# Second layer's gate and up by seven block products, with weight sums made in the first layer

## The chip, the cores and the metric

The kernel runs on 1 core of one Trainium2 chip. The metric is the device time of one execution in microseconds (us); less is better. Numbers are fp32; a matmul input is split into a high and a low fp32r part, and a product is three matmuls: high by high, high by low, low by high.

## The reference

Two layers of a diffusion transformer on 512 latent and 256 context tokens of width 1024. Each layer: modulated layer norm, one projection into four head groups (global attention, windowed attention, Fourier mix, retention), output projection, gated residual with norm; then the feed-forward part that the change touches:

```
def swiglu(h, w_gu, w_dn):
    g, u = jnp.split(h @ w_gu, 2, axis=-1)
    return (jax.nn.silu(g) * u) @ w_dn
```

h has 1024 columns, w_gu has 2 x 2816 columns, w_dn is 2816 x 1024. In the second layer only the 512 latent tokens are needed from here on.

## The kernel before, in words

Work is written per engine, and semaphores tie the engines together. SP loads weights, POOL splits them into high and low, PE (TensorE) multiplies, ACT and DVE read the results out of PSUM.

**Units and slots.** `plan` (L55) lists all weight loads in order. A unit is one load into one of the two halves of `stage` (L168); it holds four slots of 128 x 512. A unit's half is free again once all of its slots are split (`unit_release_wait`, L325). `split` (L755) runs on POOL: L757 writes the high part into a place of the ring, L760 writes stage minus high as the low part. The ring (`ring_hi`, `ring_lo`, L170) has 8 places, so slot g may be written when PE has used slot g - 8 (`ring_used`). PE waits for a slot by `w_ready`. `product` (L843 to L845) is the three matmuls; all weight products of the kernel have these lines.

**Gate and up** (`gate_up`, L1436). The 2816 columns are 22 chunks of 128 gate and 128 up columns, done in two halves of 11 (`gu0`, `gu1`), each followed by its part of the down projection (`dn0`, `dn1`). A chunk is one unit, four slots, each with two blocks of 128 of the 1024 rows of w_gu, for gate and up. In the first layer a chunk multiplies 768 tokens in two parts of 384 columns (96 matmuls); in the second 512 tokens at once (48 matmuls). Chunks 0 and 1 of `gu0` are done in parts of 256 tokens (`part`, L1468) while the norm before them ends; chunk 0 then has its own buffers (`own_hi`, `own_lo`). In the second layer tiles 2 and 3 of the tokens come first, then 4 and 5.

**Read-out.** ACT makes silu of a chunk's gate (`gate_half`, L2032; L2043), DVE multiplies it by up into `hid` (`up_half`, L2672; L2679). Chunks use two sets of PSUM banks in turn, so chunk f waits for the product of chunk f - 2. ACT and DVE split `hid` for down (L2030, L2184; `hid_high`, `hid_lows`). Between chunks DVE also adds up modulation vectors for later (`ffn_terms`, L2497; lines L2494, L2495) from `mod_stage`, loaded by ACT's queue; PE sums their columns in some chunks of the first layer.

**Order around the change.** Each engine's stream is in the order written. On SP: unit loads, each after the release of the unit two before, with bias rows in between (L668). The norm before gate and up (`norm_steps`) writes the modulated tokens of two tiles in turn into `hbuf` (L226), ACT makes `act_hi` and DVE `act_lo` (L2184) of them. Norm weights of a layer lie in rows 2 and 3 of `bc` (L227); `load_norm` (L2019) brings the second norm's after the first norm's steps (L2152).

## Time and profile before

| | |
|---|---|
| three runs, median (lowest to highest) | 1631.61 us (1630.08 to 1632.77) |
| the profiled execution, span from first to last instruction | 1629.1 us |
| median of the runs less that span | 2.5 us |
| mean granted TensorE clock | 0.999 |
| busy: PE, DVE, ACT, POOL | 1592.0, 783.9, 427.1, 855.8 us |

The profile is one execution on the core. Busy is the sum of an engine's instructions; the chain of waits is followed back from the last instruction. PE instructions overlap, so the pace of PE is read from the distance of two starts, not from the length of one. L numbers are lines of the kernel before. The profile gives the span of its execution, not its time between host marks, so the two are compared by the difference in the table.

### The profile page before, as it was taken

The page shows a single profiled execution, that of the slowest core. Times are in us where ns is not written, and L with a number is a line of the kernel's source. Part 1 is how long each engine was busy: PE and PEld are TensorE (multiplying, and loading weights), DVE is VectorE, ACT ScalarE, POOL GpSimd, SP SyncE. Part 2 cuts the span into 40 slices and gives each one's busy share as a digit, 9 for nine tenths or more (in the row PEclk, how much of TensorE's full clock was granted, in tenths as well). Part 3 has the DMA queues.
Part 4 walks back from the last instruction along what each step waited for, and adds up shares of the span by engine and source line. Part 5 has one row for each costly group of instructions (what it writes and reads, how often), then busy time and mean ns, then how long its engine had stood idle before and what let it go on. Part 6 is the DMA issues. An engine that isn't in the chain of part 4 may idle for free.

```text
span 1629.1 us, 23301 instructions
## 1 busy us (share of the span) xinstructions
PE 1592.0 (98%) x9335; PEld 1358.5 (83%) x9335; DVE 783.9 (48%) x1201; ACT 427.1 (26%) x920; POOL 855.8 (53%) x850
## 2 busy tenths in 40 slices
PE   7999999999999999999999999999999999999997
PEld 5788666778999988899999888886778888888886
DVE  4352265549663414443555396715659322520038
ACT  5512365425400011100002065216534200200011
POOL 4643044633464444544445455613485777777772
PEclk9999999999999999999999999999999999999999
DMA  9312143121453312244561121210032642233321
GB/s 343 118 52 78 41 149 118 57 78 52 119 165 92 117 40 78 67 146 124 177 210 60 66 78 53 78 52 9 15 85 74 195 142 91 90 95 101 104 91 52
DMA packets 161369, 160.89 MB, mean 99 GB/s; under 512 B 6520, under 2 KB 120296, under 8 KB 161264
## 3 DMA queue, kind: packets, MB, share of 16 engines
q1 hardware_dynamic: 140928, 121.40, 24.5%
q10 hardware_dynamic: 20336, 38.03, 7.2%
q8 instruction: 74, 1.21, 0.3%
q14 instruction: 31, 0.25, 0.0%
HBM read 157.31 MB, written 2.10 MB: 98 GB/s over the span
## 4 chain that ended last, share of the span: by engine, by line
PE 86%; DVE 7%; ACT 4%; issue 2%; DMA 1%; SPq 0%; DVEq 0%; POOL 0%; ACTq 0%
PE ps L843 24%; PE ps L845 24%; PE ps L844 24%; PE ps L1123 3%; PE ps L1147 2%; PE ps L1171 2%; ACT probs L1845 1%; DVE resid L2271 1%; DVE act_lo L2184 1%; DVE st L2212 1%; DVE ps L2193 1%; ACT hbuf L1647 1%; PE ps L966 1%; ACT probs_more L1845 1%; PE ps L927 1%
## 5 line engine op out<-in xcount | busy, mean ns | idle before, releaser
L757 POOL TENSOR_SCALAR ring_hi<-stage 128x512 fp32r<-128x512 f32 x352 | 245.3, 697 | 519.5 <-PE ps L845 450.0
L760 POOL TENSOR_TENSOR ring_lo<-stage,ring_hi 128x512 fp32r<-128x512 f32 x352 | 480.8, 1366 | 29.4
L843 PE MATMUL ps<-act_hi,ring_hi 128*128 128x384 f32 (+2 forms) x1088 | 379.1, 348 | 0.5 <-POOL ring_lo L760 0.5
L845 PE MATMUL ps<-act_hi,ring_lo 128*128 128x384 f32 (+2 forms) x1088 | 377.8, 347 | 0.0
L844 PE MATMUL ps<-act_lo,ring_hi 128*128 128x384 f32 (+2 forms) x1088 | 377.8, 347 | 0.0
L843 PE MATMUL ps<-ring_hi,act_hi 128*128 128x512 f32 (+1 forms) x711 | 280.6, 395 | 0.4 <-DVE act_lo L2184 0.4
L845 PE MATMUL ps<-ring_hi,act_lo 128*128 128x512 f32 (+1 forms) x711 | 273.5, 385 | 0.0
L844 PE MATMUL ps<-ring_lo,act_hi 128*128 128x512 f32 (+1 forms) x711 | 273.1, 384 | 0.0
L843 PEld LDWEIGHTS ps<-act_hi,ring_hi 128*128 128x128 f32 x1088 | 204.6, 188 | 13.9 <-POOL ring_lo L760 0.7
L845 PEld LDWEIGHTS ps<-act_hi,ring_lo 128*128 128x128 f32 x1088 | 204.5, 188 | 13.2
L844 PEld LDWEIGHTS ps<-act_lo,ring_hi 128*128 128x128 f32 x1088 | 204.6, 188 | 13.0
L2679 DVE TENSOR_TENSOR hid<-silu_g,ps 128x768 f32<-128x768 f32 (+1 forms) x44 | 36.1, 821 | 301.9 <-ACT silu_g L2043 301.6
L2043 ACT ACTIVATE silu_g<-ps 128x768 f32<-128x768 f32 (+1 forms) x44 | 31.1, 706 | 555.6 <-PE ps L845 525.6
L843 PEld LDWEIGHTS ps<-ring_hi,act_hi 128*128 128x128 f32 x711 | 133.7, 188 | 31.1 <-issue 4.0
L845 PEld LDWEIGHTS ps<-ring_hi,act_lo 128*128 128x128 f32 x711 | 133.5, 188 | 27.3
L844 PEld LDWEIGHTS ps<-ring_lo,act_hi 128*128 128x128 f32 x711 | 133.8, 188 | 26.3 <-issue 1.4
L770 POOL TENSOR_SCALAR probs<-probs,rden 128x768 f32<-128x768 f32 (+3 forms) x50 | 38.6, 779 | 128.9 <-DVE rden L2482 128.9
L2474 DVE TENSOR_REDUCE negmax<-ps 128x1 f32<-128x768 f32 (+4 forms) x80 | 58.0, 766 | 65.2 <-PE ps L1085 36.9
L2495 DVE SCALAR_TENSOR_TENSOR mod_acc_ffn<-mod_stage,c_silu,mod_acc_ffn 128x512 f32<-128x512 f32 x84 | 78.7, 963 | 18.8 <-DMA mod_stage<-in_w_mod_dram 17.0
L843 PE MATMUL ps<-ring_hi,hs_hi 128*128 128x512 f32 x220 | 86.6, 393 | 0.1
L845 PE MATMUL ps<-ring_hi,hs_lo 128*128 128x512 f32 x220 | 85.7, 389 | 0.0
L844 PE MATMUL ps<-ring_lo,hs_hi 128*128 128x512 f32 x220 | 85.6, 389 | 0.0
(278 smaller groups left out, 2046.1 us busy)
## 6 DMA issues: line engine op xcount, KB each, us to landing
stage<-in_w_gate_up_dram SPq DMA_DIRECT2D x88, 512.0 KB, 5.1
mod_stage<-in_w_mod_dram ACTq DMA_DIRECT2D x56, 512.0 KB, 4.2
stage<-in_w_in_dram SPq DMA_DIRECT2D x18, 1024.0 KB, 5.0
stage<-in_w_down_dram SPq DMA_DIRECT2D x16, 1024.0 KB, 5.0
stage<-in_w_mod_dram SPq DMA_DIRECT2D x12, 1024.0 KB, 5.2
start_mod<-in_w_mod_dram SPq DMA_DIRECT2D x16, 512.0 KB, 9.7
stage<-in_w_down_dram SPq DMA_DIRECT2D x8, 768.0 KB, 4.4
stage<-in_w_out_dram SPq DMA_DIRECT2D x16, 256.0 KB, 4.5
```

The lines of the kernel that those rows point to most:

```text
L757: nc.gpsimd.tensor_scalar(hi_, stage[:, par, j * 512:(j + 1) * 512], 1.0, 0.0, ALU.mult, ALU.add).then_inc(w_hi, 1)
L760: nc.gpsimd.tensor_tensor(lo_, stage[:, par, j * 512:(j + 1) * 512], hi_.bitcast(F32), ALU.subtract).then_inc(w_ready, 1)
L770: nc.gpsimd.tensor_scalar(probs_slot(2 * i + a)[:, 0:n], probs_slot(2 * i + a)[:, 0:n], rden[:, m:m + 1], 0.0, ALU.mult, ALU.add).then_inc ...
L843: nc.tensor.matmul(o, a_hi, b_hi, start=first, stop=False)
L844: nc.tensor.matmul(o, a_hi, b_lo, start=False, stop=False)
L845: return nc.tensor.matmul(o, a_lo, b_hi, start=False, stop=last)
L1123: last[a] = nc.tensor.matmul(flat[a][:, c0:c0 + m * P], qk[rows[a], b, t * P:(t + 1) * P], qk[rows[a], 2, k0 * P:(k0 + m) * P], start=True ...
L1147: mm = nc.tensor.transpose(ps[:, 4 + c, (j % 4) * P:(j % 4 + 1) * P], probs_slot(2 * i + a)[:, k * P:(k + 1) * P], ident[:, :])
L1171: mm = nc.tensor.matmul(ps[rows[a], 7, 0:P], v_attn[g][:, k, rows[a]], probs_T[1 - i % 2][:, (a * n + j) * P:(a * n + j + 1) * P], start=( ...
L2474: v.tensor_reduce(negmax[:, m:m + 1], flat[:, 0:n], AX, ALU.max, negate=True).then_inc(sem("neg_ready"), 1)
L2495: return v.scalar_tensor_tensor(acc, w, c_k, acc, ALU.mult, ALU.add)
L2679: done(v.tensor_tensor(hid[:, j, lo_col:TOK].rearrange("p (r n) -> p r n", **pat), silu_g[:, e, lo_col:TOK].rearrange("p (r n) -> p r n", ...
```

## The change

It replaces 19 of the second layer's 22 chunks of gate and up (chunks 3 to 10 of the first half and all 11 of the second), called fast chunks. A chunk's weights are a 2 x 2 block matrix (gate and up by two halves of the 1024 rows) and the tokens another (two halves of the rows by two halves of 256 tokens). Their product is formed from seven block products (Winograd's form) in place of eight, each of 4 blocks of 128 rows by 256 tokens, hence 4 x 3 matmuls of 256 columns.

- Four of the seven left factors are sums of weight blocks. POOL makes them (`weight_sums`) ahead of unit splits in the first layer's halves, from weights that SP loads for that into `pre_sum`, rows 2 and 3 of `bc`; SP stores them to DRAM (`send_sums`). The second norm's rows of the first layer are loaded only after the last store.
- A fast chunk has two units, of 4 and 3 slots (`send_fast`). ACT makes all seven high parts, DVE the low parts of slots 3 and 4, POOL the other five.
- The token sums are made by DVE (`t_sums`, `t_lows`) and ACT (`t_highs`) from `hbuf` and two more tile buffers, so `hbuf` isn't reused in that norm.
- PE's steps 4, 5 and 6 add onto PSUM banks that hold earlier products. ACT copies the first (`fast_copy`) and DVE forms the sums (`fast_half`).

```diff
+FIRST_FAST = {(DEPTH - 1, 0): 3, (DEPTH - 1, 1): 0}
+STEPS = 7
+FAST_FIRST = 4
+BY_DVE = (3, 4)
...
+def sum_units():
+    places = [UNIT0[(0, "gu0")] + f for f in range(2, HALF)] + [UNIT0[(0, "gu1")] + f for f in range(HALF)]
+    return places[:len(fast_chunks()) + 1]
...
+        def fast_left(u, i):
+            u, j = (u, {0: 0, 2: 1, 1: 2, 3: 3}[i]) if i < FAST_FIRST else (u + 1, {6: 0, 4: 1, 5: 2}[i])
+            return stage[:, u % 2, j * 512:(j + 1) * 512]
+        def fast_right(i):
+            first, second = slice(CTX, CTX + 256), slice(CTX + 256, TOK)
+            return {0: (act_hi[:, 0:4, first], act_lo[:, 0:4, first]),
+                    1: (act_hi[:, 0:4, 0:256], act_lo[:, 0:4, 0:256]),
+                    2: (act_hi[:, 4:8, 0:256], act_lo[:, 4:8, 0:256]),
+                    3: (t1_sets[:, 0, :, :], t1_sets[:, 1, :, :]),
+                    4: (act_hi[:, 4:8, first], act_lo[:, 4:8, first]),
+                    5: (t4_sets[:, 0:4, 0:256], t4_sets[:, 4:8, 0:256]),
+                    6: (act_hi[:, 4:8, second], act_lo[:, 4:8, second])}[i]
...
+            def send_sums(n):
+                if n:
+                    sp.wait_ge(sem("sums_made"), 4 * n)
+                    sp.dma_start(sums_dram[n - 1, :, :], pre_sum[:, :, :].rearrange("p b c -> p (b c)")).then_inc(sem("sums_stored"), 16)
+                if n == len(fast_chunks()):
+                    return
+                l, fh, f = fast_chunks()[n]
+                sp.wait_ge(sem("sums_stored"), 16 * n)
+                if n == 0:
+                    need(sp, "sum2", (0, 1), NT)
+                blocks = pre_sum[:, :, :].rearrange("p b (k c) -> p b k c", k=4)
+                gate, up = (gu_src(l, g, fh * HALF + f) for g in range(2))
+                sp.dma_start(blocks[:, 1, :, :], gate[:, 0:4, :]).then_inc(sem("sums_in"), 16)
+                sp.dma_start(blocks[:, 0, :, :], gate[:, 4:8, :]).then_inc(sem("sums_in"), 16)
+                sp.dma_start(pre_sum[:, 2:4, :].rearrange("p b (k c) -> p (b k) c", k=4), up).then_inc(sem("sums_in"), 16)
...
+                    def send_fast(u, f, n):
+                        first, second = (stage[:, v % 2, :].rearrange("p (b k c) -> p b k c", b=4, k=4) for v in (u, u + 1))
+                        unit_release_wait(sp, u - 2)
+                        sp.dma_start(first[:, 0, :, :], gu_src(l, 0, f)[:, 0:4, :]).then_inc(unit_in[u % 2], 16)
+                        sp.wait_ge(sem("sums_stored"), 16 * (n + 1))
+                        sp.dma_start(stage[:, u % 2, 512:2048], sums_dram[n, :, 512:2048]).then_inc(unit_in[u % 2], 16)
+                        unit_release_wait(sp, u - 1)
+                        sp.dma_start(second[:, 1, :, :], gu_src(l, 0, f)[:, 4:8, :]).then_inc(unit_in[(u + 1) % 2], 16)
+                        sp.dma_start(second[:, 2, :, :], gu_src(l, 1, f)[:, 4:8, :]).then_inc(unit_in[(u + 1) % 2], 16)
+                        sp.dma_start(stage[:, (u + 1) % 2, 0:512], sums_dram[n, :, 0:512]).then_inc(unit_in[(u + 1) % 2], 16)
...
+            def weight_sums(n):
+                pool.wait_ge(sem("sums_in"), 48 * (n + 1))
+                for m, (o, a, b, op) in enumerate(((3, 2, 3, ALU.add), (2, 1, 2, ALU.subtract), (1, 3, 1, ALU.subtract),
+                                                   (0, 0, 1, ALU.subtract))):
+                    if m:
+                        pool.wait_ge(sem("sums_made"), 4 * n + m)
+                    nc.gpsimd.tensor_tensor(pre_sum[:, o, :], pre_sum[:, a, :], pre_sum[:, b, :], op).then_inc(sem("sums_made"), 1)
+            def fast_low(l, u, g, i):
+                pool.wait_ge(ring_used, g - 7)
+                pool.wait_ge(sem("fast_hi"), slots_of((ACT_HIGH, DVE_LOW), g))
+                nc.gpsimd.tensor_tensor(ring_lo[:, g % RING, :], fast_left(u, i), ring_hi[:, g % RING, :].bitcast(F32),
+                                        ALU.subtract).then_inc(w_ready, 1)
...
+                    first = fast_part((l, seg), i)
+                    if first is not None:
+                        for j in range(first, first + n):
+                            if j not in BY_DVE:
+                                fast_low(l, u0 - (first > 0), g0 + j - first, j)
+                        g0 += n
+                        u0 += 1
+                        continue
...
+                    if u0 in sum_units()[:-1]:
+                        weight_sums(sum_units().index(u0))
...
+                def fast_chunk(g, f):
+                    c = fast_number(l, fh, f)
+                    if f >= 2:
+                        need(pe, "hid_ready", l, f0 + f - 1)
+                    elif f == 1:
+                        need(pe, "dn_read", l, 2 * len(tiles_of(l)))
+                    for i, (gu, r) in enumerate(((0, 0), (1, 0), (1, 1), (0, 1), (0, 0), (1, 0), (0, 1))):
+                        slot_wait(pe, g + i)
+                        if c == 0 and i in T_DONE:
+                            need(pe, "t_done", l, T_DONE[i])
+                        if i == 4:
+                            need(pe, "fast_copy", l, c + 1)
+                        elif i > 4:
+                            need(pe, "fast_read", l, 3 * c + i - 3)
+                        b_hi, b_lo = fast_right(i)
+                        for k in range(4):
+                            w = slice(k * P, (k + 1) * P)
+                            mm = joined(fast_bank(l, fh, f, gu, r), ring_hi[:, (g + i) % RING, w], ring_lo[:, (g + i) % RING, w],
+                                        b_hi[:, k, :], b_lo[:, k, :], i < 4 and k == 0, k == 3)
+                        mm.then_inc(ring_used, 1)
...
+            def fast_highs(l, fh, f):
+                g, u = gu_slot(l, fh, f), gu_unit(l, fh, f)
+                for i in range(STEPS):
+                    if i in (0, FAST_FIRST):
+                        unit_wait(act, u + i // FAST_FIRST)
+                    act.wait_ge(ring_used, g + i - 7)
+                    a.activation(ring_hi[:, (g + i) % RING, :], fast_left(u, i), ACT.Copy).then_inc(sem("fast_hi"), 1)
+                    if i == 0 and f and is_fast(l, fh, f - 1):
+                        fast_copy(l, fh, f - 1)
+            def fast_copy(l, fh, f):
+                c = fast_number(l, fh, f)
+                act.wait_ge(ring_used, gu_slot(l, fh, f) + 1)
+                need(act, "fast_read", l, 3 * c)
+                a.activation(one[:, :], fast_bank(l, fh, f, 0, 0), ACT.Copy).then_inc(sem("fast_copy"), 1)
+            def t_highs(l, ns):
+                for n in ns:
+                    i, j = T_ORDER[n]
+                    need(act, "t_ready", l, n + 1)
+                    src, dst = t_source(i, j), t_part(fast_right(i)[0], j)
+                    a.activation(dst, src, ACT.Copy).then_inc(sem("t_hi"), 1)
...
+                if (l, fh) == (DEPTH - 1, 0):
+                    t_highs(l, range(4))
                 for f in range(HALF):
+                    if f < HALF - 1 and is_fast(l, fh, f + 1):
+                        fast_highs(l, fh, f + 1)
                     if f == HALF - 1:
...
+                        if is_fast(l, fh, f):
+                            send_fast(u, f0 + f, fast_number(l, fh, f))
+                            continue
+                        unit_release_wait(sp, u - 2)
+                        send_gu(u, f0 + f)
                         if f in (1, 2) and seg == "gu0":
...
+                if fh == 0 and is_fast(l, 1, 0):
+                    fast_highs(l, 1, 0)
...
+                if l < DEPTH - 1:
+                    act.wait_ge(sem("sums_stored"), 16 * len(fast_chunks()))
+                    load_norm(l, ln2_w, ln2_b)
...
+            def t_sums():
+                k0, k1 = slice(0, 512), slice(512, D)
+                for j in range(2):
+                    done(v.tensor_tensor(h_more[j][:, k1], h_more[j][:, k1], h_more[j][:, k0], ALU.subtract), "t_ready")
+                for j in range(2):
+                    done(v.tensor_tensor(h_more[j][:, k0], h_more[j][:, k0], hbuf[:, j, k0], ALU.subtract), "t_ready")
+                for j in range(2):
+                    ins = v.tensor_tensor(hbuf[:, j, k0], hbuf[:, j, k0], h_more[j][:, k1], ALU.add)
+                done(ins, "t_ready")
+            def t_lows(l):
+                k0, k1 = slice(0, 512), slice(512, D)
+                done(v.tensor_tensor(hbuf[:, :, k1], hbuf[:, :, k1], hbuf[:, :, k0], ALU.subtract), "t_ready")
+                for n, (i, j) in enumerate(T_ORDER):
+                    need(dve, "t_hi", l, n + 1)
+                    if i == 5:
+                        dve.wait_ge(ring_used, gu_slot(l, 0, 1))
+                    hi_, lo_ = (t_part(x, j) for x in fast_right(i))
+                    done(low(lo_, t_source(i, j), hi_), "t_done")
+            def fast_lows(l, fh, f, which):
+                u, g, c = gu_unit(l, fh, f), gu_slot(l, fh, f), fast_number(l, fh, f)
+                for i in which:
+                    dve.wait_ge(ring_used, g + i - 7)
+                    need(dve, "fast_hi", l, STEPS * c + i + 1)
+                    done(low(ring_lo[:, (g + i) % RING, :], fast_left(u, i), ring_hi[:, (g + i) % RING, :]), "fast_lo")
+            def fast_half(l, fh, f, between):
+                g, c = gu_slot(l, fh, f), fast_number(l, fh, f)
+                _, g2, u1, u2 = (fast_bank(l, fh, f, gu, r) for gu in range(2) for r in range(2))
+                more = f < HALF - 1
+                def after(i):
+                    dve.wait_ge(ring_used, g + i + 1)
+                after(2)
+                need(dve, "fast_copy", l, c + 1)
+                done(v.tensor_tensor(both[:, :], one[:, :], u2, ALU.add), "fast_read")
+                done(v.tensor_tensor(one[:, :], both[:, :], u1, ALU.add), "fast_read")
+                after(3)
+                done(v.tensor_tensor(u2, one[:, :], g2, ALU.add), "fast_read")
+                if more:
+                    fast_lows(l, fh, f + 1, BY_DVE)
+                between()
+                after(5)
+                link(v.tensor_tensor(u1, both[:, :], u1, ALU.add))
+                after(6)
+                done(v.tensor_tensor(g2, both[:, :], g2, ALU.add), "fast_gate")
...
+                if (l, fh) == (DEPTH - 1, 0):
+                    t_sums()
                 for f in range(HALF):
+                    if is_fast(l, fh, f):
+                        fast_half(l, fh, f, first_slices if f == HALF - 1 else lambda: ffn_terms((l, fh), f))
+                        need(dve, "silu_ready", l, fh * HALF + f + 1)
+                        chunk(f)
+                        continue
                     if f == HALF - 1:
```

Not shown: the bookkeeping of slots by kind (`slot_wait`: a fast slot whose low DVE makes is waited for by `fast_lo`, any other by `w_ready`), `joined` (as `product`, without the group check), and the order in which `t_highs` go on ACT: the first four before chunk 0's silu, two after it. In the last chunk of a half DVE does the first `hid_lows` (1 in the first half, 4 in the second) between step 3's and step 5's sums.

## Rows read from the trace of the kernel before

**Rows 1.** The page: busy us by engine, and the chain that ended last.
```profile
PE 1592.0 (98%) x9335; PEld 1358.5 (83%) x9335; DVE 783.9 (48%) x1201; ACT 427.1 (26%) x920; POOL 855.8 (53%) x850
...
PE 86%; DVE 7%; ACT 4%; issue 2%; DMA 1%; SPq 0%; DVEq 0%; POOL 0%; ACTq 0%
```

**Rows 2.** Windows (us): length, busy by engine, PE clock, DMA share, GB/s.
```profile
690.00:880.00 190.00, 190.00 (x1119) 189.86 (x1118) 92.44 (x109) 11.98 (x15) 89.66 (x88) 1.00 0.48 148
1291.00:1379.00 88.00, 88.00 (x390) 72.84 (x389) 19.78 (x23) 6.33 (x12) 66.67 (x68) 1.00 0.40 120
1440.00:1561.00 121.00, 121.00 (x536) 100.19 (x535) 15.82 (x21) 9.06 (x16) 86.25 (x90) 1.00 0.33 94
```

**Rows 3.** Timeline of ACT, second layer's second half: start, length, what.
```profile
1473.18 0.60 ACT L2043 ACTIVATE silu_g<-ps 128x512 f32<-128x512 f32 x1 [10.28 <-PE ps L845]
...
1549.34 0.60 ACT L2043 ACTIVATE silu_g<-ps 128x512 f32<-128x512 f32 x1 [10.28 <-PE ps L845]
```

**Rows 4.** Timeline of PE, second and 49th of a row of 256 column matmuls.
```profile
1268.96 0.28 PE L844 MATMUL ps<-act_lo,own_hi 128*128 128x256 f32 x1
...
1274.59 0.28 PE L843 MATMUL ps<-act_hi,ring_hi 128*128 128x256 f32 x1
```

**Rows 5.** Groups by line, 1291 to 1561: count, busy us, mean ns, idle before.
```profile
L760 POOL TENSOR_TENSOR ring_lo<-stage,ring_hi 128x512 fp32r<-128x512 f32 x101 | 134.8, 1334 | 8.5
L757 POOL TENSOR_SCALAR ring_hi<-stage 128x512 fp32r<-128x512 f32 x100 | 66.8, 668 | 63.0 <-PE ps L845 62.1
L2184 DVE TENSOR_TENSOR hs_lo<-hid,hs_hi 128x512 fp32r<-128x512 f32 x19 | 22.1, 1163 | 23.8 <-ACT hs_hi L2030 23.6
L2030 ACT ACTIVATE hs_hi<-hid 128x512 fp32r<-128x512 f32 x19 | 11.8, 630 | 36.6 <-PE ps L845 36.5
```

**Rows 6.** DMA issues, 1440 to 1561: count, size, median landing; L728's extremes, whole span.
```profile
stage<-in_w_gate_up_dram SPq DMA_DIRECT2D x16, 512.0 KB, 5.0
stage<-in_w_down_dram SPq DMA_DIRECT2D x2, 1024.0 KB, 4.9
DMA to landing us min/median/max: 3.8/5.1/7.0
```

**Rows 7.** Timeline of DVE: a first-layer low, then the second layer's first chunks.
```profile
410.42 2.20 DVE L2184 TENSOR_TENSOR act_lo<-hbuf,act_hi 128x1024 fp32r<-128x1024 f32 x1
...
1267.99 1.42 DVE L2184 TENSOR_TENSOR act_lo<-hbuf,act_hi 128x512 fp32r<-128x512 f32 x2 [0.77 <-ACT act_hi L1660]
1275.49 0.69 DVE L2679 TENSOR_TENSOR hid<-silu_g,ps 128x512 f32<-128x512 f32 x1 [6.08 <-ACT silu_g L2043]
1276.21 1.50 DVE L2494 TENSOR_SCALAR bc<-mod_stage,c_silu 128x512 f32<-128x512 f32 x1
1277.75 0.75 DVE L2495 SCALAR_TENSOR_TENSOR bc<-mod_stage,c_silu,bc 128x512 f32<-128x512 f32 x1
...
1281.97 2.07 DVE L2495 SCALAR_TENSOR_TENSOR bc<-mod_stage,c_silu,bc 128x512 f32<-128x512 f32 x2
```

**Rows 8.** Timeline where the first half goes over to down.
```profile
1378.30 0.39 PE L843 MATMUL ps<-ring_hi,hs_hi 128*128 128x512 f32 x1
...
1379.92 1.91 DVE L2184 TENSOR_TENSOR hs_lo<-hid,hs_hi 128x512 fp32r<-128x512 f32 x2
...
1381.25 0.47 PE L843 MATMUL ps<-ring_hi,hs_hi 128*128 128x512 f32 x1
```

**Rows 9.** First layer: POOL's lows (group, 436 to 880; one), chunk products, a store.
```profile
L760 POOL TENSOR_TENSOR ring_lo<-stage,ring_hi 128x512 fp32r<-128x512 f32 x105 | 145.0, 1381 | 8.8
...
400.49 2.13 POOL L760 TENSOR_TENSOR ring_lo<-stage,ring_hi 128x512 fp32r<-128x512 f32 x1
...
706.66 0.95 DVE L2679 TENSOR_TENSOR hid<-silu_g,ps 128x768 f32<-128x768 f32 x1 [12.22 <-ACT silu_g L2043]
...
880.23 0.96 DVE L2679 TENSOR_TENSOR hid<-silu_g,ps 128x768 f32<-128x768 f32 x1 [5.37 <-ACT silu_g L2043]
...
out_dram<-resid SPq DMA_DIRECT2D x3, 512.0 KB, 2.7
```

More of the change, by code:

```diff
@@ L47, with is_fast, fast_number, fast_chunks @@
 START_TILES = [2, 3, 0, 4, 1, 5]
-def segment(key):
-    return [-4] * 2 + [4] * 7 if key == (1, "win") else SEGMENTS[key[1]]
+FIRST_FAST = {(DEPTH - 1, 0): 3, (DEPTH - 1, 1): 0}
+STEPS = 7
+FAST_FIRST = 4
+BY_DVE = (3, 4)
+def is_fast(l, fh, f):
+    return f >= FIRST_FAST.get((l, fh), HALF)
+def fast_number(l, fh, f):
+    return sum(is_fast(l, h, j) for h in range(2) for j in range(HALF) if (h, j) < (fh, f))
+def fast_chunks():
+    return [(l, h, f) for l in range(DEPTH) for h in range(2) for f in range(HALF) if is_fast(l, h, f)]
+def gu_units(l, fh, f):
+    return sum(2 if is_fast(l, fh, j) else 1 for j in range(f))
+def segment(key):
+    if key == (1, "win"):
+        return [-4] * 2 + [4] * 7
+    if key[1][:2] == "gu":
+        fast = [is_fast(key[0], int(key[1][2]), f) for f in range(HALF)]
+        return sum(([FAST_FIRST, STEPS - FAST_FIRST] if one else [4] for one in fast), [])
+    return SEGMENTS[key[1]]
+def fast_part(key, i):
+    if key[1][:2] != "gu":
+        return None
+    place = i - FIRST_FAST.get((key[0], int(key[1][2])), HALF)
+    return None if place < 0 else FAST_FIRST * (place % 2)
 def plan():
-    order = []
+    order, kinds = [], []
     for l in range(DEPTH):
@@ L845, in product, with joined @@
                 return nc.tensor.matmul(o, a_lo, b_hi, start=False, stop=last)
+            def joined(o, a_hi, a_lo, b_hi, b_lo, first, last):
+                nc.tensor.matmul(o, a_hi, b_hi, start=first, stop=False, skip_group_check=True)
+                nc.tensor.matmul(o, a_hi, b_lo, start=False, stop=False, skip_group_check=True)
+                return nc.tensor.matmul(o, a_lo, b_hi, start=False, stop=last, skip_group_check=True)
             def keep_clock(bank, n):
@@ L2067, in gate_half @@
                             hid_high(l, 2 * fh, j)
-                    chunk(f, g0 + 4 * f + 4, fh * HALF + f - 1 if f >= 2 else None)
+                    chunk(f, gu_slot(l, fh, f) + 4, fh * HALF + f - 1 if f >= 2 else None)
+                    if (l, fh, f) == (DEPTH - 1, 0, 0):
+                        t_highs(l, range(4, 6))
                     load_mods(f)
@@ L2711, in down_low @@
                         link(half_stats(t, 0, 0))
+                if fh == 0 and is_fast(l, 1, 0):
+                    fast_lows(l, 1, 0, BY_DVE)
                 if fh == 0:
```

125 lines of the change are left out of this document (91 added, 34 removed).

## The prediction

> **What bounds the kernel now.** I read the page's busy times and its chain first, then a table by stage, then the timelines of the stretches that change. TensorE is busy 98% of the span and carries 86% of the chain [rows 1]: time is gained only where its stream gets shorter, lost where another engine makes it wait. The changed stretches are the second layer's two gate and up halves, and in both TensorE is busy for the whole window at granted clock 1.00 (the 2.4 GHz level), POOL for 71 to 76% [rows 2]. A chunk there takes 10.88 us: eight silus from 1473.18 to 1549.34 are seven equal periods [rows 3], and a chunk is 48 matmuls of 512 columns, so 226.7 ns each. In the first layer's halves TensorE is full too; POOL works 89.66 of 190 us there [rows 2], so it has room for the weight sums.
>
> **The products.** A fast chunk issues 7 x 4 x 3 = 84 matmuls of 256 columns for 48 of 512. The trace has such matmuls, each with its own weights, at the start of this layer's gate and up: from 1268.96 to 1274.59 are 47 intervals, 120 ns each [rows 4]. Their weight loads are in that pace. So 84 x 0.120 = 10.08 us against 10.88: 0.80 us less, although columns fall by an eighth (1.36 us), since each matmul costs 13.3 ns beyond its columns and there are 36 more. Chunks 3 to 10 of the first half and all 11 of the second are fast: 19 x 0.80 = **15.2 us gained**.
>
> The Trainium skill ("TensorE: Matmul & The Clock Gate", Back-to-back issue gap) gives an isolated gap of columns/2.4 + 2.5 ns. By that 84 are 9.2 us and 48 are 10.4 us, an estimate of 1.2 us a chunk and 22.5 us in all. The rows show 120 and 226.7 ns for this stream, so the trace does not agree and decides.
>
> **Who prepares the operands.** Before, POOL did both parts of 4 slots a chunk, 4 x (0.67 + 1.33) = 8.0 us [rows 5]. Now ACT copies 7 highs, 7 x 0.63 = 4.4, plus a quarter-size PSUM copy and silu 0.60 [rows 3]: under 5.5 us of 10.08. POOL subtracts 5 lows: 6.7 us. DVE has 2 lows (2 x 1.16), five combinations of 256 columns (0.4 each at most; half the 0.69 of the 512 wide read of PSUM in rows 7), the product 0.69, in the first half some terms: 5.0 to 7 us. None is the bound by its sum. The combinations of one chunk end before their PSUM halves are wanted (step 5 wants step 2's sums, 2.9 us later).
>
> **The loop that can be the bound.** Slots 0 to 3 of a fast chunk are one stage buffer. Its next load may start only when these four are split, and PE's step 4 needs a copy that ACT makes behind the *next* chunk's first high, that is behind that landing. So landing leads to landing: ACT high 0.63, three POOL lows 3 x 1.33 with 0.1 of semaphores = 4.8 us (DVE's low of slot 3 ends about then), then the load. It is 1 MB in two DMAs; two 512 KB ones of a unit land in 5.0 us at the median, 3.8 to 7.0, a single 1 MB one in 4.9 [rows 6]. I take 5.2. Sum 10.0, against 10.08 of PE: level. Bounds: 3.8 gives 8.6 (nothing lost), 7.0 gives 11.8 (1.7 a chunk). The second half starts with the buffer loaded during down, and its second load goes out when slot 3's low is done, 7.7 us into chunk 0, and lands 2.9 us into chunk 1. PE stops only if a landing comes more than 4.7 us in (the copy is wanted at 5.76, a high and the copy take 1.0), so small drifts cost nothing. I take 1.0 us in all.
>
> Port contention goes against this. A DVE subtraction of 512 columns with both inputs in SBUF takes 0.71 us beside an idle POOL (two in 1.42, rows at 1267.99), and 1.16 on average [rows 5, 7]; one of 1024 columns took 2.20 beside a busy POOL [rows 7]. The Trainium skill ("SBUF — State Buffer", Who interferes with whom) has it as a lock: a DVE instruction with two SBUF inputs and a GpSimd one that reads SBUF block each other for a whole instruction. The trace agrees; it adds nothing to the sum. One of the loop's three POOL lows at the 2.13 that a blocked one took [rows 9] makes the loop 10.8.
>
> **Entry of the first fast chunk.** DVE must make the token sums before it: six 512 wide, from the last low's end at 1269.4 (4.3 to 7.0 us); after chunk 0's product, one 1024 wide, four lows 512 wide and two 1024 wide (7.0 to 11.3 us). Behind them wait chunk 0's terms, chunk 1's product, its terms (2.3 + 0.7 + 2.1 [rows 7]) and the low of slot 3. That low ends between 1289.0 and 1294.7; the next load (5.1) and its high and copy (1.0) follow, to 1295.1 or 1300.8. PE starts the chunk at 1291.2 and wants the copy at 1297.0. Stall 0 to 3.8 us; I take **2.0**.
>
> **Ends of the halves.** Silu now waits for a last DVE sum (0.4 and a hand-over), so the last product comes 0.5 us later. In the first half slot 1's low comes right after it, and PE waited for it already: 2.95 us between its first matmul and that one, for 12 matmuls worth 2.72 [rows 8]. In the second, four 1.16 us lows stand ahead of the last sums on DVE and push them past the chunk's end by about 1.5. 0.5 each, **1.0**; bounds 0 and 3.
>
> **First layer.** Each of 19 sets adds to POOL four 512 wide instructions, 4 x 1.38 = 5.5 us [rows 9], to SP one 1 MB store and three loads of 1 MB together, with SP waiting for the sums and for the store. Behind SP's waits stand the next gate and up unit and bias rows; behind POOL's wait for the loads the next unit's splits, and PE behind them. Set to set: store 4 (512 KB land in 2.7 [rows 9]), loads 6, sums 5.8 = 15.8 us; POOL's work a chunk is 8.3 + 5.5 = 13.8. PE's chunks come every 17.36 (ten from 706.66 to 880.23 [rows 9]), and the ring lets POOL lead by 7 slots of 4.34 us, so a late set is covered. DMA share was 0.48 [rows 2] and would be about 0.87 if each byte cost the same, so latencies will grow. Bounds of a set: 2.7 + 3.8 + 5.2 = 11.7; 5.4 + 7.8 (the last of three loads issued 0.8 later) + 4 x 2.13 = 21.7. I charge **0.4**. The second norm's rows load after the last store, over 60 us before their use: nothing.
>
> **Sum.** 15.2 - 1.0 - 2.0 - 1.0 - 0.4 = 10.8. The span was 1629.1, so 1618.3; the runs' median stands 2.5 above it, so **1620.8 us**.
>
> **Rivals.**
> *The buffer loop paces the chunks.* At 10.5 us a chunk the 19 save 7.2, less entry and ends 3.0: 1627.4. For it: the sum above is level with no margin, and the lock. Against: landings hold at 5.0 in this very half [rows 6], and a load of long rows should not be slower than one of short ones. Chance 0.25 (1624 to 1631).
> *All of it hides:* 15.2, 1616.4. For: POOL leaves DVE free more often now that ACT takes the highs. Chance 0.10.
> *The sums' round trip starves the first layer* (slower than before). SP's store, its wait, the loads and POOL's sums are one serial loop. At 21.7 us a set PE loses 4.3 a chunk once POOL's lead of 30 us is spent: 8 sets 35 - 30 = 5, 11 sets 48 - 30 = 18, so 23 us: 1644. It decides from about 21 us a set. For: DMA share 0.87. Against: store and load never run together in it. Chance 0.08.
> *The change doesn't do what it says:* the shorter matmuls lose their pace among step changes and operands from six places, say 128 ns: 10.75 a chunk, 2.5 saved, 1629 to 1635. Rows 4 speak against. Chance 0.05.
> *Each matmul costs its columns alone:* 19 x 48 x 512/2400 less 19 x 84 x 256/2400 is 24.3 us, 1611. The rows' 13.3 ns exclude it nearly: 0.02. (It is close to the isolated-gap rule of the Trainium skill, "TensorE: Matmul & The Clock Gate", Back-to-back issue gap.)
>
> **How the numbers follow.** Forecast (1617.5 to 1623.5) 0.50. The rest: 0.25, 0.10, 0.08, 0.05, 0.02. The range 1616 to 1629 takes in the hidden case and most of the loop's, and leaves out the first-layer case and the tails. 0.2% is 3.3 us, about what a measurement tells from no change. Faster (under 1628.3): 0.50 + 0.10 + 0.02 + 0.20 of the loop's + 0.01 of the slower matmuls' = 0.83. Same: 0.05 + 0.04 = 0.09. Slower 0.08.
>
> **What would show it.** Right: silu periods of 10.1 us in fast chunks, 256 column matmuls 120 ns apart within steps; one wait of PE of about 2 us on ACT's copy in the first half's chunk 3; first-layer periods unchanged at 17.36 on average; POOL busy some 104 us more there (19 x 5.5), less in the second layer. Wrong: periods of 10.4 or more with PE waiting at step 4 in each chunk (the loop); first-layer periods above 17.4 on average with PE waiting for POOL's lows (the sums); intervals over 0.12 us inside a step (the products).

## The result, and the profile after

Four runs of the changed kernel have a median of 1639.9 us (1633.5 to 1642.8), against 1631.0 (1630.1 to 1632.8) for the kernel before: ratio 1.0049 [1.0028, 1.0070]. It is slower by 9 us where 1620.8 was forecast. The profiled execution is the quickest of the four, with a span of 1631.3 us; the spans of the others are 1636.8 to 1640.6. So this trace shows only part of the loss, and a second profile of the same kernel (after_again, span 1643.2) stands beside it. Below, the quickest trace is the first of the two.

The page after, answering to [rows 1]:

```profile
PE 1583.2 (97%) x10019; PEld 1382.2 (85%) x10019; DVE 931.7 (57%) x1347; ACT 510.4 (31%) x1078; POOL 965.1 (59%) x869
...
PE 73%; DVE 11%; DMA 6%; ACT 5%; issue 3%; POOL 2%; SPq 0%; ACTq 0%; DVEq 0%; POOLq 0%
```

TensorE is less busy in time, as meant, but its share of the chain fell from 86% to 73%, and DMA, 1% before, has 6%. The windows of [rows 2], after:

```profile
690.00:880.00 190.00, 187.93 (x1099) 187.84 (x1098) 111.45 (x107) 11.29 (x14) 141.99 (x119) 0.99 0.72 231
1291.00:1379.00 88.00, 81.37 (x641) 79.47 (x640) 63.41 (x76) 38.31 (x74) 58.80 (x40) 0.98 0.59 195
1440.00:1561.00 121.00, 119.42 (x954) 116.91 (x952) 70.08 (x97) 54.82 (x103) 83.26 (x59) 1.00 0.52 170
```

PE was busy for the whole of each before. Now it stops in all three, in the first layer too, where the DMA share went from 0.48 to 0.72 and 148 GB/s became 231 (a packet counts where it starts, so a short window can show a share over 1). What it waited for, in the second profile (line, releaser, total us, times, longest):

```profile
PE ps L1035 <- ACT one L2262: 11.2, 8, 4.2
...
PE ps L1079 <- DVE mod_acc_ffn L2752: 4.3, 1, 4.3
...
PE ps L1035 <- POOL ring_lo L936: 1.6, 1, 1.6
```

L1035 is a fast chunk's first matmul line, L2262 the copy that step 4 wants, L1079 the column sums of modulation vectors. The profile of the quickest run has 6.4 us in 6 waits, 2.1 and 1.5 in these lines.

**The products** are as forecast. The pace inside a step, and the silus of the second half, answering to [rows 4] and [rows 3]:

```profile
1523.42 0.28 PE L1037 MATMUL ps<-act_hi,ring_lo 128*128 128x256 f32 x1
1523.54 0.28 PE L1035 MATMUL ps<-t_sets,ring_hi 128*128 128x256 f32 x1
1523.66 0.28 PE L1036 MATMUL ps<-t_sets,ring_hi 128*128 128x256 f32 x1
```

```profile
1458.49 0.60 ACT L2286 ACTIVATE silu_g<-ps 128x512 f32<-128x512 f32 x1 [1.34 <-DVE ps L2980]
...
1552.76 0.60 ACT L2286 ACTIVATE silu_g<-ps 128x512 f32<-128x512 f32 x1 [1.74 <-DVE ps L2980]
```

120 ns a matmul, across the change of step as well; but nine silu periods are 94.27 us, 10.47 each. The 19 fast chunks of this trace take 202.7 us where 19 x 10.08 is 191.5 and the old chunks took 206.7: of 15.2 us, 4.0 are left. In after_again they take 208.7 us, longer than the old ones: nothing is left.

**The first layer's second half** ran from 706.66 to 880.23 before [rows 9], 173.57 us. After:

```profile
705.81 0.95 DVE L2989 TENSOR_TENSOR hid<-silu_g,ps 128x768 f32<-128x768 f32 x1 [12.22 <-ACT silu_g L2286]
...
883.16 0.95 DVE L2989 TENSOR_TENSOR hid<-silu_g,ps 128x768 f32<-128x768 f32 x1 [5.37 <-ACT silu_g L2286]
```

177.35, and 181.63 in the second profile. The chain of waits of the quickest run shows the place:

```profile
820.27 7.03 DMA mod_stage<-in_w_mod_dram
...
827.40 1.10 DVE mod_acc_ffn L2752
...
828.52 0.99 DVE mod_acc_ffn L2752
...
829.56 1.05 PE ps L1079 x8
```

The load of the last terms took 7.03 us, these came late, and PE's column sums behind them. Before, the load in this place was issued at 822.68 and the terms started at 826.60, 3.9 us later. The rows of before, then the window 820 to 825 of before and of after:

```profile
822.68 2.37 ACTq L2057 DMA_DIRECT2D mod_stage<-in_w_mod_dram  x2
...
826.60 1.54 DVE L2495 SCALAR_TENSOR_TENSOR mod_acc_ffn<-mod_stage,c_silu,mod_acc_ffn 128x512 f32<-128x512 f32 x2 [1.96 <-DMA mod_stage<-in_w_mod_dram]
```

```profile
820.00:825.00 5.00, 5.00 (x31) 5.00 (x30) 4.41 (x4) 0.00 (x0) 2.73 (x3) 1.00 0.24 59
```

```profile
820.00:825.00 5.00, 5.00 (x31) 5.00 (x30) 1.86 (x2) 0.00 (x0) 2.93 (x3) 1.00 1.14 335
```

Before, the 16 matmuls of the column sums ran as one row (first fence below); in the second profile the last eight waited, and the granted clock followed (windows with the columns of [rows 2]):

```profile
827.38 1.86 PE L887 MATMUL ps<-ones,mod_acc_ffn 128*128 128x1 f32 x16
```

```profile
827.61 0.95 PE L1079 MATMUL ps<-ones,mod_acc_ffn 128*128 128x1 f32 x8
832.90 1.44 PE L1079 MATMUL ps<-ones,mod_acc_ffn 128*128 128x1 f32 x6 [4.33 <-DVE mod_acc_ffn L2752]
```

```profile
825.00:830.00 5.00, 3.56 (x25) 3.48 (x23) 2.49 (x2) 0.00 (x0) 4.77 (x5) 1.00 0.98 320
830.00:835.00 5.00, 2.10 (x9) 2.11 (x10) 2.85 (x4) 0.81 (x1) 3.87 (x3) 0.54 0.43 134
835.00:840.00 5.00, 5.00 (x17) 5.00 (x17) 3.14 (x5) 0.00 (x0) 0.00 (x0) 0.50 1.02 371
840.00:845.00 5.00, 5.00 (x29) 5.00 (x28) 1.34 (x2) 0.00 (x0) 1.92 (x2) 0.93 0.37 122
```

At 835 to 840 PE is busy throughout but runs 17 matmuls where 840 to 845 has 29: half speed, the 1.2 GHz level. One wait of 4.3 us costs 8.1 in all; in the quickest run 2.1 us cost 3.8. In the trace of before the last of those terms ended at 828.14 (826.60 and 1.54), and PE wanted it about 0.2 us later, half-way through its row of 16.

**The buffer loop,** ACT's and SP's timelines in the second half of the quickest run:

```profile
1524.20 0.63 ACT L2253 ACTIVATE ring_hi<-stage 128x512 fp32r<-128x512 f32 x1 [3.25 <-DMA stage<-weight_sums]
1524.74 0.36 ACT L2262 ACTIVATE one<-ps 128x256 f32<-128x256 f32 x1
...
1535.46 0.63 ACT L2253 ACTIVATE ring_hi<-stage 128x512 fp32r<-128x512 f32 x1 [4.10 <-DMA stage<-weight_sums]
1536.00 0.37 ACT L2262 ACTIVATE one<-ps 128x256 f32<-128x256 f32 x1
```

```profile
1529.27 0.37 SPq L876 DMA_DIRECT2D stage<-in_w_gate_up_dram  x1
1529.68 0.91 SPq L878 DMA_DIRECT2D stage<-weight_sums  x1
1532.23 0.37 SPq L880 DMA_DIRECT2D stage<-in_w_gate_up_dram  x1
```

From one landing to the next is 11.26 us: 5.1 until the buffer is free, then 6.2 for the load, with the second unit's load started 3.0 us behind it. This is one of the two longest of the half: its nine periods from landing to landing are 10.15 to 11.27, 10.63 on average, with 5.1 until the buffer is free nearly every time and loads of 5.1 to 5.3 us (six) or 5.6 to 6.2 us (four). Each time the copy for step 4 comes right after the first high of the next chunk, so after the landing.

**The entry of the first fast chunk,** ACT's timeline:

```profile
1290.22 0.60 ACT L2286 ACTIVATE silu_g<-ps 128x512 f32<-128x512 f32 x1 [7.35 <-DVE bc L2752]
1293.21 0.38 ACTq L2300 DMA_DIRECT2D mod_stage<-in_w_mod_dram  x1
1293.69 3.75 ACT L2253 ACTIVATE ring_hi<-stage 128x512 fp32r<-128x512 f32 x7 [2.87 <-DVE bc L2752]
...
1303.77 0.63 ACT L2253 ACTIVATE ring_hi<-stage 128x512 fp32r<-128x512 f32 x1 [5.85 <-DMA stage<-weight_sums]
1304.31 0.36 ACT L2262 ACTIVATE one<-ps 128x256 f32<-128x256 f32 x1
```

ACT stood 7.35 and 2.87 us in its own stream, waiting to issue modulation loads until DVE had used the ones before; DVE was at the token sums first, then at chunk 1's product and terms. ACT's highs, the next load and the copy all came late. That chunk took 14.79 us, 3.4 us of it at granted clock 0.50, and began 1.7 late.

### The profile page after: what moved, and what is told of

It reads as the page before. It is cut to its first block, busy times and chain, and to the rows that moved or that the text cites. A ratio compares the mean times of both kernels' runs of the same rounds, so it can differ in the third digit from the quotient of the medians.

```text
span 1631.3 us, 25476 instructions
## 1 busy us (share of the span) xinstructions
PE 1583.2 (97%) x10019; PEld 1382.2 (85%) x10019; DVE 931.7 (57%) x1347; ACT 510.4 (31%) x1078; POOL 965.1 (59%) x869
## 4 chain that ended last, share of the span: by engine, by line
PE 73%; DVE 11%; DMA 6%; ACT 5%; issue 3%; POOL 2%; SPq 0%; ACTq 0%; DVEq 0%; POOLq 0%
PE ps L1029 18%; PE ps L1031 18%; PE ps L1030 18%; DMA stage<-weight_sums 3%; PE ps L1315 3%; PE ps L1339 2%; DMA mod_stage<-in_w_mod_dram 2%; PE ps L1035 2%; PE ps L1037 2%; PE ps L1036 2%; POOL ring_lo L936 2%; DVE act_lo L2441 2%; PE ps L1363 2%; ACT probs L2059 1%; DVE st L2469 1%
## 5 line engine op out<-in xcount | busy, mean ns | idle before, releaser
L1029 PE MATMUL ps<-act_hi,ring_hi 128*128 128x384 f32 (+2 forms) x784 | 261.4, 333 | 0.5 <-POOL ring_lo L920 0.5
L1031 PE MATMUL ps<-act_hi,ring_lo 128*128 128x384 f32 (+2 forms) x784 | 260.3, 332 | 0.0
L1030 PE MATMUL ps<-act_lo,ring_hi 128*128 128x384 f32 (+2 forms) x784 | 260.2, 332 | 0.0
L930 POOL TENSOR_TENSOR pre_sum<-pre_sum 128x512 f32<-128x512 f32 x76 | 114.5, 1506 | 62.7 <-DMA pre_sum<-in_w_gate_up_dram 58.2
L1029 PEld LDWEIGHTS ps<-act_hi,ring_hi 128*128 128x128 f32 x784 | 148.1, 189 | 2.1 <-POOL ring_lo L920 0.7
L1031 PEld LDWEIGHTS ps<-act_hi,ring_lo 128*128 128x128 f32 x784 | 148.0, 189 | 1.3
L1030 PEld LDWEIGHTS ps<-act_lo,ring_hi 128*128 128x128 f32 x784 | 148.0, 189 | 1.2
L1035 PE MATMUL ps<-act_hi,ring_hi 128*128 128x256 f32 x380 | 108.8, 286 | 8.2 <-ACT one L2262 6.4
L1037 PE MATMUL ps<-act_hi,ring_lo 128*128 128x256 f32 x380 | 107.6, 283 | 0.0
L1036 PE MATMUL ps<-act_lo,ring_hi 128*128 128x256 f32 x380 | 107.6, 283 | 0.0
```

What stands on the lines that cost most here:

```text
L930: nc.gpsimd.tensor_tensor(pre_sum[:, o, :], pre_sum[:, a, :], pre_sum[:, b, :], op).then_inc(sem("sums_made"), 1)
L1029: nc.tensor.matmul(o, a_hi, b_hi, start=first, stop=False)
L1030: nc.tensor.matmul(o, a_hi, b_lo, start=False, stop=False)
L1031: return nc.tensor.matmul(o, a_lo, b_hi, start=False, stop=last)
L1035: nc.tensor.matmul(o, a_hi, b_hi, start=first, stop=False, skip_group_check=True)
L1036: nc.tensor.matmul(o, a_hi, b_lo, start=False, stop=False, skip_group_check=True)
```

## The experiments

Three groups of runs, each with the kernel before on the same chip (medians 1631.2, 1631.3 and 1631.0). All start from the changed kernel.

**after_again:** no edit, a second look.

> The changed kernel unaltered, for its spread over executions and a second trace. Theory A (in the first layer the traffic of the weight sums delays the loads of modulation weights, PE then waits for DVE's sums of them, and falls to the 1.2 GHz level for 3.4 us): executions between 1633 and 1643 us, and the lower the granted clock the longer; a trace of a longer execution has two to four such waits in the first layer's second half, where the first trace had one (2.1 us and 3.4 us at the lower level). Theory B (the spread comes from the fast chunks' loop of loads): the first layer is as in the first trace and fast chunks 3 to 10 of the first half are longer.

1641.9 us (1638.2 to 1645.4, 6 runs), ratio 1.0062 [1.0048, 1.0076]. This is the size of the loss; its waits are shown above. Neither theory has it alone: the first layer has one wait, not two to four, but of 4.3 us where the quickest trace had 2.1, and the half takes 4.3 us longer than in that trace; the fast chunks take 6.0 us longer.

**one_set:** only the first of 19 sets of sums is loaded, made and stored, and every fast chunk reads that one.

```diff
 def send_sums(n):
+    if n > 1: return
...
-    if n == len(fast_chunks()):
+    if n:
         return
...
-    sp.dma_start(stage[:, u % 2, 512:2048], sums_dram[n, :, 512:2048])
+    sp.dma_start(stage[:, u % 2, 512:2048], sums_dram[0, :, 512:2048])
 def weight_sums(n):
+    if n: return
```

> Only the first of the 19 sets of weight sums is loaded, made and stored; every fast chunk reads that one set (so most products are of wrong sums). Theory A: the first layer's second half goes back to the pace of the kernel before (silu to silu from chunk 0 to 10 in 173.6 us, changed kernel 177.3), the spread goes, and the time is 1628 to 1630 us. Theory B: the first layer gains the 3.7 us of the first trace at most, spread stays, median 1635 or more.

1634.9 (1630.8 to 1637.4, 11 runs), 1.0020 [1.0012, 1.0029]. The first layer's second half is back at 173.55 us without a wait at L1079. 6.9 us of after_again's time are in the making of the sums, loads and stores included. Theory A had the place, but its 1628 to 1630 left out the faults of the second layer, which stay.

**dma_only:** the loads and stores of the sets stay, POOL's sums go.

```diff
-    sp.wait_ge(sem("sums_made"), 4 * n)
+    sp.wait_ge(sem("sums_in"), 48 * n)
 def weight_sums(n):
+    return
```

> All 19 loads and stores of the weight sums stay, POOL's four instructions a set are left out (what is stored is not the sums). Theory A (traffic alone): as the changed kernel, median 1637 to 1641 us, waits of PE for modulation sums in the first layer stay. Rival C (POOL's sums and DVE's modulation terms block each other at the SBUF port, and DVE is late for that): the waits go, median 1628 to 1632 us.

1639.3 (1637.5 to 1644.7, 6 runs), 1.0056 [1.0043, 1.0069]. The wait at L1079 is there, 3.73 us, and the half takes 179.98. So the transfers alone bring the wait: it needs neither POOL's 5.5 us a set nor a lock of DVE by POOL. They may add a little, since the last two terms take 2.10 us in the changed kernel and 1.54 here; the time differs from after_again's by 2.5 us, within their spread, and no run makes the sums without the transfers.

**copy_first:** ACT copies PSUM for step 4 before it waits for the next load.

```diff
 for i in range(STEPS):
+    if i == 0 and f and is_fast(l, fh, f - 1):
+        fast_copy(l, fh, f - 1)
     if i in (0, FAST_FIRST):
         unit_wait(act, u + i // FAST_FIRST)
...
-    if i == 0 and f and is_fast(l, fh, f - 1):
-        fast_copy(l, fh, f - 1)
```

> ACT's copy of a fast chunk's first bank goes ahead of its wait for the next chunk's load. Theory D (the loop of loads reaches PE only through that copy at step 4): waits at step 4 go, fast chunks come every 10.08 us but for the first, 6.5 us less than the changed kernel and 2 to 4 us more at the first fast chunk: 8 to 10 us below the changed kernel's median. Rival E (the loop, at 10.3 us or more, moves the wait to step 0 of the next chunk, where its first slot is wanted): fast chunks at 10.3 us and more stay, gain under 3 us.

1638.7 (1635.0 to 1638.9, 5 runs), 1.0038 [1.0026, 1.0050]. Nine of the second half's 11 chunks take 10.08 us, the others 10.36 and 10.15: there the loop reached PE through the copy alone. In the first half 6.4 us of waits in 4 places remain, and the wait at L1079 is 4.3. There the copy stands behind other waits of ACT: for the first fast chunk behind the issue of a modulation load that waits 5.25 us for DVE's terms, later behind a silu that waits 4 to 5 us for DVE's last sums. So the run gains 3 us only, where 8 to 10 were expected.

**late_sum:** the column sums of one item are issued a chunk later.

```diff
 def ffn_sum_chunk(half, n):
-    return last + (3 if (half, n) == ((0, 0), 0) else 2)
+    return last + (3 if (half, n) in (((0, 0), 0), ((0, 1), 5)) else 2)
```

> PE's column sums of the last modulation item of the first layer's second half come one chunk later; the traffic of the weight sums stays. Theory A (the traffic hurts by that one wait and the lower level behind it): no wait there, silu to silu of that half 173.6 us, 5 to 8 us below the changed kernel: 1633 to 1636. Rival F (the traffic also costs elsewhere in that half, or the wait moves to a later place): pace stays over 175 us, gain under 3 us.

1634.3 (1630.5 to 1636.6, 12 runs), 1.0018 [1.0009, 1.0027], with all traffic in place. The clock and PE in the windows shown for after_again:

```profile
825.00:830.00 5.00, 5.00 (x34) 5.00 (x33) 3.19 (x4) 0.00 (x0) 4.83 (x5) 1.00 0.72 211
830.00:835.00 5.00, 5.00 (x31) 5.00 (x30) 3.48 (x5) 0.81 (x1) 3.39 (x3) 1.00 0.65 211
835.00:840.00 5.00, 5.00 (x31) 5.00 (x30) 2.38 (x4) 0.00 (x0) 1.91 (x2) 1.00 0.81 283
```

The half takes 173.55. One number in the order of work gives back 7.5 us of after_again's time (5.6 of the first four runs' 1639.9), as much as taking the sums away.

**copy_silu:** the copy goes just ahead of the silu of the chunk before, far from any load. Its two old places go, and that for the second half's chunk 0 stands ahead of the loop.

```diff
 for f in range(HALF):
...
+    if f < HALF - 1 and is_fast(l, fh, f + 1):
+        fast_copy(l, fh, f + 1)
     chunk(f, ...)
```

> ACT's copy for chunk f+1 goes ahead of the silu of chunk f. Theory G (in the first half, where ACT's copy stood behind a silu that DVE's terms had delayed, that order is all that was left of waits in chunks 4 to 10): these come every 10.1 us, 2 to 3 us less than with the copy ahead of the load alone; the first fast chunk keeps its 5 us. About 1636. Rival H (DVE itself is full in that half, about 10.7 us of work and waits a chunk): the waits move to the sums of PSUM halves at steps 5 and 6 and stay 0.5 to 1 us a chunk.

1637.6 (1635.2 to 1641.2, 6 runs), 1.0041 [1.0029, 1.0054]. The waits for the copy are gone, and others stand in their place, one step on:

```profile
PE ps L1035 <- DVE one L2971: 6.9, 4, 3.5
...
PE ps L1079 <- DVE mod_acc_ffn L2752: 5.4, 1, 5.4
```

DVE's sums that step 5 adds to are late, all four times in the first half, where DVE has the modulation terms as well. The waits moved one step on, as rival H says.

**all_three:** late_sum and copy_silu, and in the first half's three old chunks DVE does the terms before the product, so that ACT's loads are released sooner.

```diff
 # up_half, chunks that are not fast
+    if (l, fh) == (DEPTH - 1, 0):
+        ffn_terms((l, fh), f)
     need(dve, "silu_ready", l, fh * HALF + f + 1)
...
-    ffn_terms((l, fh), f)
+    if (l, fh) != (DEPTH - 1, 0):
+        ffn_terms((l, fh), f)
```

> Late column sums, the copy ahead of silu, and, in the second layer's first half, DVE's modulation terms of chunks 0 to 2 ahead of these chunks' products and of the token sums' second part, so that ACT is not held by its loads of modulation weights when it should split for the first fast chunk. Theory: the wait at the first fast chunk falls from 5 or 6 us to under 2, and the time to 1622 to 1627 us, below the kernel before. Rival (the token sums alone are too long for DVE): 3 us or more stay at the first fast chunk, 1627 to 1632.

1626.4 (1624.9 to 1628.3, 7 runs), 0.9973 [0.9963, 0.9984]: faster than the kernel before by 4.9 us in that group. The changed stretches, to set beside those above:

```profile
690.00:880.00 190.00, 190.00 (x1119) 189.78 (x1118) 113.45 (x109) 12.11 (x15) 141.44 (x121) 1.00 0.74 232
1291.00:1379.00 88.00, 83.33 (x675) 82.55 (x675) 65.33 (x79) 36.51 (x70) 59.91 (x43) 0.98 0.59 195
1440.00:1561.00 121.00, 121.00 (x969) 118.95 (x968) 78.16 (x103) 55.58 (x103) 84.23 (x61) 1.00 0.52 171
```

The first layer and the second half are full again, the latter with 11 chunks of 10.08. The first half still has 7.0 us over 8 x 10.08. The first fast chunk's wait is 1.0 us, as the theory has it, but the second's is 2.6.

**all_three_one_set:** one_set with all_three's copy and entry order.

> The copy and term order of all_three with only one set of weight sums made (every fast chunk reads it, so most products are of wrong sums). If the first layer's traffic costs nothing once the column sums come later, this is within 2 us of all_three; if it still costs, it is more than 3 us faster.

1628.4 (1624.1 to 1629.1, 11 runs), 0.9979 [0.9970, 0.9987]. Without 18 of the 19 sets it is no faster than all_three (2.0 us slower, for which no trace shows a cause): once the column sums have room, the sets cost the first layer nothing that shows.

**no_terms:** all_three with the first half's terms cut to 8 of 512 columns.

```diff
+w = slice(0, 8 if half == (DEPTH - 1, 0) else 512)
-ins = term(acc[:, o, :], mod_stage[:, u % 2, k, :], ...
+ins = term(acc[:, o, w], mod_stage[:, u % 2, k, w], ...
```

> all_three with the modulation terms of the second layer's first half cut to 8 of 512 columns (the second gate is wrong then); their loads stay. Theory I (what is left of waits in that half, 4.2 us and a fall of the clock in the trace of all_three, is DVE's load: its terms take 1.67 us each beside POOL): fast chunks 3 to 10 all at 10.1 us, 3 to 5 us faster than all_three, 1621 to 1623. Rival J (the waits come from the loads or from the copy): they stay, within 1 us of all_three.

1622.8 (1621.5 to 1624.0, 5 runs), 0.9951 [0.9938, 0.9963], 3.6 us less than all_three. PE's waits for DVE fall from 4.7 to 1.5 us; 2.5 us over 10.08 a chunk remain, so theory I's "all at 10.1" didn't come. The terms of all_three, then of no_terms, groups of the first half (count, busy us, mean ns), and the timelines of DVE and POOL in no_terms, with two terms beside an idle POOL first:

```profile
L2752 DVE SCALAR_TENSOR_TENSOR bc<-mod_stage,c_silu,bc 128x512 f32<-128x512 f32 x11 | 18.3, 1665 | 0.4
```

```profile
L2752 DVE SCALAR_TENSOR_TENSOR bc<-mod_stage,c_silu,bc 128x8 f32<-128x8 f32 x11 | 13.0, 1185 | 0.4
```

```profile
1286.48 0.49 DVE L2752 SCALAR_TENSOR_TENSOR bc<-mod_stage,c_silu,bc 128x8 f32<-128x8 f32 x2
...
1313.88 1.15 DVE L2751 TENSOR_SCALAR bc<-mod_stage,c_silu 128x8 f32<-128x8 f32 x1
1315.07 1.21 DVE L2752 SCALAR_TENSOR_TENSOR bc<-mod_stage,c_silu,bc 128x8 f32<-128x8 f32 x1
...
1313.71 2.55 POOL L936 TENSOR_TENSOR ring_lo<-stage,ring_hi 128x512 fp32r<-128x512 f32 x2 [0.57 <-ACT ring_hi L2253]
```

Eight columns still take 1.2 us beside POOL, where two took 0.49 together without it. The last one ends at 1316.28, as POOL's second low does (1316.26): most of such a term's time is waiting for POOL, not work. With terms of 8 columns DVE is still held for 13.0 us, so what the terms cost in all may be more than 3.6 us.

**low4_pool:** POOL instead of DVE makes slot 4's low in the first half.

```diff
-BY_DVE = (3, 4)
+BY_DVE = ((3,), (3, 4))
```

> all_three with the low part of slot 4 in the first half on POOL (6 lows) and one on DVE. Theory I: DVE is relieved by 1.4 us a chunk and the waits of chunks 4 to 8 go, 2 to 3 us faster than all_three, 1623 to 1625. Rival K (POOL, at 8.6 us and more a chunk, is then the later one, or the lock gives the time back): within 1 us of all_three or slower.

1626.2 (1624.0 to 1628.7, 6 runs), 0.9971 [0.9960, 0.9983]: all_three's time. Two waits of 4.5 us together stand where there were four of 4.7. The work taken from DVE gave no time back; by which way the gain was lost, POOL's longer list or the lock, the run doesn't tell.

**copy_silu_late:** all_three without the entry order.

> all_three without the moved modulation terms of chunks 0 to 2: what their place costs. Theory (ACT's loads wait for them and its splits for the first fast chunk stand behind): PE's wait for POOL's first low at chunk 3 (1.5 us) comes back and the one at chunk 4 is as long as in copy_silu (3.5 us): 3 to 5 us slower than all_three, 1630 to 1631. Rival: it is the number of DVE instructions that counts, not their place: within 1.5 us.

1628.8 (1627.0 to 1630.6, 11 runs), 0.9987 [0.9978, 0.9996]. The entry order is worth 2.4 us (3 to 5 were expected), and the copy's place, from late_sum to this kernel, 5.5.

**entry_copy_late:** all_three with copy_first's place of the copy.

> all_three with the copy ahead of the next chunk's load but behind silu. If the copy's place relative to silu matters (DVE's lateness reaches PE at step 4 by silu and copy), 1 to 3 us slower than all_three; if DVE's own sums at step 5 are the limit either way, within 1 us, the waits one step earlier.

1628.6 (1626.7 to 1631.6, 11 runs), 0.9986 [0.9977, 0.9995], 2.2 us over all_three. PE waits for the copy six times, 6.2 us, where all_three has 4.7 for DVE's sums. (The two traces are the slowest run of this kernel and the quickest of all_three, so they may overstate the difference.)

## Why the prediction was wrong

From after_again's 1641.9 the medians go down in steps: column sums later 1634.3, copy's place 1628.8, entry 1626.4, terms 1622.8. The forecast was 1620.8. The steps are each one comparison, all over two groups of runs (their kernels before differ by 0.3 us at most); by the spread of the runs the two small ones are good to about 2 us and the two large ones to about 4.

Three terms of the sum were too small, and none explains the miss alone: with the first layer whole again (late_sum) the time is still 1634.3. By the traces, quickest and after_again, in us beyond what was charged: first layer 3.4 and 7.7, loop 5.5 and 10.1, entry 4.4 and 5.7. The spans were 13.0 and 24.9 over the forecast's 1618.3.

- **Products (15.2 gained): right.** 120 ns in every unstalled step, chunks of 10.08 us, all 11 of them in all_three's second half.
- **First layer (0.4 charged): the step whose mechanism failed; it lost 3.8 and 8.1 us, and late_sum gives back 7.5.** The text asked whether POOL's lead covers a set, and it does: no profile has PE waiting there for POOL's lows. But it followed the new transfers to one queue only. "Latencies will grow" stands in it, and was not carried to the modulation loads of ACT's queue, whose chain (load, DVE terms, column sums on PE) had 0.2 us to spare in the trace of before. Their median landing in 700 to 880 went only from 4.2 to 4.6 us and the longest from 6.6 to 7.7, but the load that the last terms need took 7.03 where it had taken 3.9. The clock then about doubled the loss. dma_only shows that it needs no work of POOL; one_set and late_sum each bring back 173.55.
- **Loop (1.0 charged): the mechanism right, the size wrong, and the largest of the three.** Of the quickest trace's fast chunks after the first, the excess over 10.08 is 6.5 us, all at step 4; of after_again's it is 11.1. The text put the loop at 10.0, level with PE, and let small drifts cost nothing; from landing to landing it was 10.63 on average in the quickest trace's second half. Most loads took the 5.2 us forecast and four 5.6 to 6.2; the buffer was free after 5.1 where 4.8 was taken, with POOL's lows 1.44 where 1.33 was. Whether the second unit's load beside it lengthens the first, no run tests. All of it was within the bounds given. The place of the copy made each late landing a wait; moving it is worth 5.5 us. In the first half the copy also waited for DVE by way of silu (copy_first), which the text didn't have.
- **Entry (2.0 charged): the wait came, its price was 6.4 us** in the quickest trace (14.79 less 10.08, and 1.7 of late start). The text looked at DVE's queue and left out ACT's: ACT waits for DVE's terms before it issues a load, and behind that wait stood a silu and seven highs. The entry order gives back 2.4, and 1.7 us of the 6.4 are the clock (3.4 us at half speed); the rest wasn't taken apart. In after_again the same reckoning gives 7.7.
- **Ends (1.0 charged): about right.** PE waits 1.2 us for the lows at the first half's end, and some 0.5 at the second's.
- **POOL (104 us more):** 76 sums of 1.51 us are 114.5 in the quickest trace, a tenth over the forecast.

Of the rivals, the one that was slower than before (the sets' round trip) had the place, the first layer, and the sets as the cause, but not the path: PE never waited there for POOL's lows. The loop rival (10.5 a chunk, 1627.4) describes the second half well, 10.47 between silus. The range failed because the first layer was allowed to lose only through POOL, and because the loop and a loss in the first layer were rivals in it and never came together.

Open: why the spread between runs grew (9 us here, 3 before); it goes with the length of the waits and of the low clock after them, but no run sets these, and like waits had different ends (see the last section). Nor is the last 7.0 us of the first half divided between DVE's terms, its lows and the late start; a run without POOL beside DVE wasn't made.

## What to carry to other kernels

Before adding traffic to a full stretch, list every queue that loads in it and read the slack of each chain that ends at the bounding engine: here a chain with 0.2 us to spare broke, though the new work itself was covered. A loop that comes out level with the bounding engine has no margin: reckon its spread as a loss. An operation that reads early data should not stand in its engine's stream behind a wait for a load, or behind an issue that itself waits: the copy's place was worth 5.5 us and the entry's 2.4. When a change with a sound gain comes out slower, look for such places before undoing it: three edits of order turned +9 us into -4.9.

## What the runs showed of the hardware

**A stop of PE of about 2 us cost its own length or nearly twice that.** Waits of 2.1 and 4.3 us in the first layer went with 3.4 and 10.2 us at granted clock 0.50 (partly within the wait), for 3.8 and 8.1 us lost in all. All 14 waits of 2.64 us or more in the feed-forward stretches, over all traces, had such a low stretch with them or right behind. Of waits of 1.7 to 2.63 us some had one (1.81 in low4_pool, 1.92 in after_again) and some had none (2.13 in after_again, 1.67 and 2.08 in entry_copy_late). The closest pair is the second fast chunk's wait for DVE's sums, 2.64 us in all_three and 2.63 in all_three_one_set; the window behind each:

```profile
1313.00:1318.00 5.00, 5.00 (x32) 5.00 (x31) 4.70 (x4) 1.67 (x3) 5.00 (x4) 0.66 0.37 127
```

```profile
1315.00:1320.00 5.00, 5.00 (x44) 5.00 (x43) 4.89 (x4) 1.42 (x3) 5.00 (x4) 1.00 0.35 121
```

The matmuls started in 5 us are 32 in one and 44 in the other.

**DVE beside POOL waits whole instructions.** A term of 512 columns took 0.75 us alone [rows 7] and 1.67 on average in all_three's first half. With 8 columns it took 1.19 on average there, the one shown ending with POOL's instruction, and about 0.25 beside an idle POOL. A TENSOR_SCALAR of 8 columns, with one streamed input, took 1.15 us and ended at 1315.03, about where the first of POOL's pair did (1313.71 and half of 2.55). The Trainium skill ("SBUF — State Buffer", Who interferes with whom) has a DVE instruction with two SBUF inputs contend, by an exclusive lock, with a GpSimd one that reads SBUF; for the terms with two inputs the trace agrees.

**A median hid the landings that counted.** Over 190 us the DMA share went from 0.48 to 0.72 (231 GB/s) and the median landing of the modulation loads by 0.4 us only. But the share came in bursts: it was 1.14 at 820 to 825, where the load of 7.03 us was issued, and 0.24 there before, where the one of 3.9 us was. Loads of 6.3 to 6.6 us stood in the trace of before too, in places where PE didn't wait for them.
